# Transposes of a unit's probabilities moved from the head of a step into the middle of its projection piece, in a two-block transformer kernel

## The chip, the cores and the metric

The kernel runs on one core of one Trainium2 chip. The metric is the device time of one execution in microseconds (us), here the median of 3 runs. A core has five engines that run their own instruction streams in order and wait for each other through semaphores: TensorE (PE in the rows; PEld is its weight load), VectorE (DVE), ScalarE (ACT), GpSimd (POOL) and the queues that issue DMA (SP above all).

## What is computed

Two blocks run one behind the other on a sequence of 512 tokens with 1024 features, each of two layers. The first block (feed-forward, pool, Fourier and differential-attention mixer, feed-forward) isn't touched by the change. A layer of the second block, `hybrid_layer`, cut to what matters:

```python
h = rms_norm(x, norm_g)
proj = einsum('btd,de->bte', h, w_in)      # a_q a_k a_v a_g, b_q b_k b_v b_g, m_q m_g
qa, ka = rope(rms_norm(a_q)), rope(rms_norm(a_k))      # 6 heads of 64
oa = moba_attention(qa, ka, a_v)
ob = dilated_attention(qb, kb, b_v)                    # 6 heads
om = memory_attention(qm, km, m_v)                     # 4 heads over 256 memory rows
y = concatenate([oa * silu(a_g), ob * silu(b_g), om * silu(m_g)])
return x + einsum('bte,ed->btd', y, w_out)
```

At 512 tokens both masked kinds of attention come down to scores plus an additive mask, a softmax over the keys, and a product with the values.

## The kernel before

All activations are held feature-major in SBUF. Every large product is made of three matmuls of split fp32 (`three`, lines L458, L459, L460: high by high, high by low, low by high), each 128 rows by 512 tokens. The weights come as a stream of panels of 128 x 2048 through two slots: the DMA fills `raw`, ScalarE copies it into `w_hi` (L945), GpSimd subtracts that into `w_lo` (L450), TensorE waits for the quarters of a panel.

The second block's attention is a software pipeline, `run_stages`. The heads go by groups (stages): stage 1 holds the memory heads, stages 2 to 7 a pair of heads each. A stage has 8 steps. A unit is one block of 128 queries for two heads: the memory stage has 8 units, one in each step; a pair stage has 4, of 128, 256, 384 and 512 keys, which begin in the steps 0, 2, 4 and 6. Each engine walks the same steps in order, and in a step does different parts of different units:

- TensorE, `attention_step`: the scores of this step's unit (L755); the outputs of a group of four units that began three steps ago or more (`LAG_OUT`, L767); the transposes of the unit that began two steps ago (`LAG_TR`, L805; 2, 4, 6 or 8 of them of 128 x 128), into PSUM banks of their own; then `produce(s)`, the step's share of the projections of later groups: four times `three`, 12 matmuls, and in the steps 2 and 3 two matmuls more that sum squares (L840, L841).
- ScalarE, `attention_step`: the copy of the transposed probabilities out of PSUM into `pt` (L1232), which waits for the transposes; in a pair stage the scaling of the probabilities into `att2` (L1240), for the unit that began one step ago (`LAG_ATT`); the exponentials (L1252) of this step's unit; then, in certain steps, copies of queries and keys with their squares (`key_out` in step 0, `query_out` in step 7), the split of a weight panel (L945), square roots (L969, L971), and silu (L1220, L1275). Exponential, root and silu need a table load of their own between them.
- VectorE: the row maximum of the scores (L1638, or L1645 with the mask), the reciprocals (L1667), in the memory stage the scaling into `att2` (L1671), the rotation, the norm of queries and keys, and the gates.

What orders the units is written out by hand as waits. In the memory stage the scores of a unit (L755) wait for the exponentials of the unit before (`t_exp`), which read the same two PSUM banks; in a pair stage they wait for its maximum (`t_max`). The first pair unit behind the memory stage waits for `t_exp` too. In all stages the transposes wait for `t_att`, the copy on ScalarE waits for the transposes (`t_tr`), and the outputs wait for the copy (`t_thi`).

In the stages 1 to 5 `produce` projects gate and value (steps 0 to 3) and query and key (steps 4 to 7) of groups ahead in halves of a chunk, `halves`. In stage 6 there is only gate and value left, in quarters (6 matmuls a step); in stage 7 `beside_last` begins the output projection, and four more steps, `tail`, end the pipeline.

Of the 32 units of a layer, 23 have their transposes in the stages 1 to 5: 8 memory units, and 15 of pairs (the fourth unit of the pair in stage 5 has its transposes in step 0 of stage 6). With two layers that is 46.

Of the kernel before, what the change touches and what calls it, by code (L numbers as in the profile page):

```python
# [152 lines left out]
def ends_group(u):  # L153
    return u % TB == TB - 1
# [58 lines left out]
def build(nc, x, mem, stream, vecs, consts, dist, masks, recip, rope, out):  # L213
    ctx = ExitStack()
    with ctx:  # L215
# [97 lines left out]
        def const(i):  # L313
            return cst[:, i * P:(i + 1) * P]
# [140 lines left out]
        def _(pe):  # L455
# [314 lines left out]
            def attention_step(here, before, s, produce):  # L770
                unit = lagged(here, before, s, 0)
                if unit:
                    stage, u = unit
                    if s == 0 and not here.memory:
                        pe.wait_ge(hn_out, GROUPS * here.l + here.gi + 1)
                    if u and stage.memory:
                        pe.wait_ge(t_exp, stage.u0 + u)
                    elif not stage.memory:
                        pe.wait_ge(t_exp if u == 0 and before.memory else t_max, stage.u0 + u)
                    scores(stage, u).then_inc(t_scores, 1)  # L780
                unit = lagged(here, before, s, LAG_OUT)
                if unit and ends_group(unit[1]):
                    stage, u = unit
                    pe.wait_ge(t_thi, stage.u0 + u + 1)
                    if not stage.memory:
                        pe.wait_ge(v_thi, 7 * stage.l + stage.gi)
                    elif u >= TB:
                        pe.wait_ge(t_y, stage.outs0 + 1)
                    outputs(stage, u).then_inc(t_o, 1)
                unit = lagged(here, before, s, LAG_TR)  # L790
                if unit:
                    stage, u = unit
                    pe.wait_ge(t_att, stage.u0 + u + 1)
                    if not stage.memory:
                        pe.wait_ge(t_thi, stage.u0 + u)
                    elif u >= 2:
                        pe.wait_ge(t_thi, stage.u0 + u - 1)
                    for h in range(2):
                        for kb in range(stage.widths[u] // P):
                            if stage.memory:  # L800
                                n = 256 * h + P * kb
                                dst, src = ps[:, 2 + u % 2, n:n + P], att2[:, h, 256 * (u % 2) + P * kb:256 * (u % 2) + P * kb + P]
                            else:
                                dst, src = ps[:, 2 + h, P * kb:P * kb + P], att2[:, h, P * kb:P * kb + P]
                            mm = pe.transpose(dst, src, const(C_ID))  # L805
                    mm.then_inc(t_tr, 1)
                if produce:
                    produce(s)
                if here and not here.memory and s == 3:
                    pe.wait_ge(v_in, 7 * here.l + here.gi)  # L810
                    pe.wait_ge(t_y, GROUPS * here.l + here.gi)
                    for tb in range(TB):
                        mm = pe.transpose(ps[:, 5, P * tb:P * tb + P],
                                          hraw[:, 0, P * tb:P * tb + P], const(C_ID))
                    mm.then_inc(v_tr, 1)
# [12 lines left out]
            def producer(l, gi):  # L828

                base = BASE2 + LAYER2_PANELS * l  # L830
                G = GROUPS * l + gi + 1
                p_gv = base + 2 * (gi + 1) + 1
                p_qk = base + 2 * (gi + 2)
                more = gi + 2 < GROUPS
                halves = [range(KB // 2), range(KB // 2, KB)]
                quarters = [range(KB // 4 * i, KB // 4 * (i + 1)) for i in range(4)]

                def mean(j):
                    pe.wait_ge(hn_lo, 12 * l + 2 * (gi - 1) + j + 1)
                    pe.matmul(ps[:, 7, :], half_r[:], sq_hi[:, j, :], start=True, stop=False)  # L840
                    pe.matmul(ps[:, 7, :], half_r[:], sq_lo[:, j, :], start=False, stop=True).then_inc(hn_mm, 1)  # L841

                def step(s):
                    if gi == 1 and s == 0:
                        pieces(p_gv - 1, 1, 4, range(KB))
                    if s == 0 and not more:
                        pe.wait_ge(hn_in, 2 * G + 1)
                    if s == 2:
                        pe.wait_ge(hn_in, 2 * G + 2)
                    if not more:  # L850
                        pieces(p_gv, s // 4, (6, 4)[s // 4], quarters[s % 4])
                    elif s < 4:
                        pieces(p_gv, s // 2, (7, 4)[s // 2], halves[s % 2])
                    else:
                        if s == 6:
                            pe.wait_ge(v_in, 7 * l + gi + 1)
                        pieces(p_qk, s // 2 - 2, (6, 4)[s // 2 - 2], halves[s % 2])
                    if s == 2:
                        if more:
                            pe.wait_ge(gate_raw, 7 * l + gi + 1)  # L860
                        mean(0)
                    if s == 3:
                        pe.wait_ge(hn_ms, 2 * G + 1)
                        mean(1)
                return step

            def stack2(l):
                n = 3 * LAYERS + l
                p0 = BASE2 + LAYER2_PANELS * l
                g0 = GROUPS * l  # L870
                pe.wait_ge(memh_ready, 8 * (l + 1))
                for c in range(4):
                    pe.wait_ge(x_ready, 8 * n + DONE_ORDER.index(c) + 1)
                    mem_chunk(c, p0, mh_hi, mh_lo, 256)
                for j in range(2):
                    head_mean(g0, j, 256)
                pe.wait_ge(h_ready, 8 * n + KB)
                mem_chunk(0, p0 + 2, h_hi, h_lo, T)
                pe.wait_ge(square_sum, n + 1)
                mm = pe.matmul(ps[:, 6, :], const(C_MEAN), y[:, 0, :], start=True, stop=True)  # L880
                if l == 0:
                    mm = pe.matmul(ps[:, 4, :], const(C_MEAN), prob2[:, 1, :], start=True, stop=True)
                mm.then_inc(mean_ready, 1)
                mem_chunk(1, p0 + 2, h_hi, h_lo, T)
                pe.wait_ge(hn_ms, 2 * g0 + 2)
                head_mean(g0 + 1, 0, T)
                pe.wait_ge(v_in, 7 * l + 1)
                mem_chunk(2, p0 + 2, h_hi, h_lo, T)
                head_mean(g0 + 1, 1, T)
                pe.wait_ge(scale_in, l + 1)  # L890
                for c in range(2):
                    for tb in range(2):
                        mm = pe.transpose(ps[:, 4, 256 * tb + P * c:256 * tb + P * c + P],
                                          hraw[:, c, P * tb:P * tb + P], const(C_ID))
                mm.then_inc(v_tr, 1)
                mem_chunk(3, p0 + 2, h_hi, h_lo, T)
                pieces(p0 + 4, 0, 6, range(KB))
                pe.wait_ge(hn_out, g0 + 2)
                pe.wait_ge(v_thi, 7 * l + 1)
                def tail(s):  # L900

                    if s > 3:
                        return
                    g = s // 2
                    if s == 0:
                        pe.wait_ge(t_max, UNITS2 * (l + 1))
                    for i in range(4) if s % 2 == 0 else range(4, KB - 1):
                        part(p0 + 2 * GROUPS, i // 2)
                        pe.wait_ge(y_ready, 8 * l + i + 1)
                        project(0, g, 0, Y_ORDER[i], i)  # L910

                def beside_last(s):

                    if s >= 2:
                        part(p0 + 2 * GROUPS + 1, s // 2 - 1)
                        pe.wait_ge(y_ready, 8 * l + s - 1)
                        for g in range(2):
                            project(1, g, 1, Y_ORDER[s - 2], s - 2)

                run_stages(l, attention_step, producer, beside_last, tail)  # L920
                project_out(p0 + 2 * GROUPS, 0, lambda i: pe.wait_ge(y_ready, 8 * l + i + 1), Y_ORDER,
                            (KB - 1, STEPS - 2, 0, 0))
# [1008 lines left out]
```

## Time and profile before

| | |
|---|---|
| Median of 3 runs | 2494.14 us (2491.28 to 2494.87) |
| The profiled execution: span, the only time recorded for it | 2491.6 us |
| TensorE matmuls busy | 2430.0 us, 98% of the span |
| ScalarE busy | 1008.0 us, 40% |
| VectorE busy | 1176.3 us, 47% |
| GpSimd busy | 1121.9 us, 45% |
| Second block's pipelines | about 1910 to 2142 us, and 2219 to 2452 us |

The table is a mean over the whole program, four fifths of which is the first block. No time of the profiled execution is recorded beside its span of 2491.6 us, which lies 2.5 us under the median of the runs. In the rows below, a time is the start of an instruction from the start of the span, and the next number is how long it took. A matmul's own time (0.39) is its latency; what it costs in a stream is the distance of its start to the next one's start.

### The profile page before, as it was taken

What the parts mean: (1) busy time and instruction counts of PE and PEld (TensorE: products, weight loads), DVE (VectorE), ACT (ScalarE), POOL (GpSimd) and SP (SyncE); (2) the same over time, 40 slices, a digit from 0 to 9 for tenths busy, and PEclk for the clock granted to TensorE, in tenths of its full rate; (3) what the DMA queues carried; (4) which work ended last, traced back from release to release, by engine and by line L of the source; (5) the groups of instructions that cost most, each with busy time, mean ns of one, the idle gap of its engine ahead of it and who ended that gap; (6) DMA issues with size and microseconds to landing.
All of it is one profiled execution on the core that took longest, in us unless ns stands there. A gap on an engine that the chain in (4) does not pass through costs nothing.

```text
span 2491.6 us, 30091 instructions
## 1 busy us (share of the span) xinstructions
PE 2430.0 (98%) x10934; PEld 1922.1 (77%) x10934; DVE 1176.3 (47%) x1805; ACT 1008.0 (40%) x1545; POOL 1121.9 (45%) x828
## 2 busy tenths in 40 slices
PE   9999999999999999999999999999999998999988
PEld 7888888668888888888888668888887676776756
DVE  6444115574555105555025665555036655466552
ACT  5333223453222124222133544222235877357772
POOL 5455445325554544555445425555444233343333
PEclk9999999999999999999999999999999999999999
DMA  4222223203222222222223212222232222132212
GB/s 174 101 87 98 102 102 117 85 34 112 90 101 101 93 93 102 94 91 101 102 85 134 72 55 94 101 101 87 99 135 96 78 85 64 68 109 66 85 64 85
DMA packets 37529, 233.18 MB, mean 94 GB/s; under 512 B 5184, under 2 KB 5312, under 8 KB 10816
## 3 DMA queue, kind: packets, MB, share of 16 engines
q1 hardware_dynamic: 36000, 226.51, 26.3%
q10 hardware_dynamic: 1440, 5.45, 0.6%
q8 instruction: 60, 0.98, 0.2%
q14 instruction: 29, 0.24, 0.0%
HBM read 223.55 MB, written 2.10 MB: 91 GB/s over the span
## 4 chain that ended last, share of the span: by engine, by line
issue 58%; POOL 42%; POOLq 1%
POOL w_lo L450 42%; POOLq L444 0%; POOLq L448 0%; POOLq L215 0%; POOLq L450 0%; POOLq L1922 0%
## 5 line engine op out<-in xcount | busy, mean ns | idle before, releaser
L450 POOL TENSOR_TENSOR w_lo<-raw,w_hi 128x512 fp32r<-128x512 f32 x824 | 1121.7, 1393 | 1369.1 <-ACT w_hi L945 1369.0
L458 PE MATMUL ps<-h_hi,w_hi 128*128 128x512 f32 x2304 | 916.4, 398 | 17.1 <-DVE h_lo L1368 10.8
L945 ACT ACTIVATE w_hi<-raw 128x1024 fp32r<-128x1024 f32 x412 | 413.7, 1053 | 1206.6 <-PE ps L460 1199.8
L460 PE MATMUL ps<-h_hi,w_lo 128*128 128x512 f32 x2304 | 900.2, 391 | 0.0
L459 PE MATMUL ps<-h_lo,w_hi 128*128 128x512 f32 x2304 | 899.6, 390 | 0.0
L458 PEld LDWEIGHTS ps<-h_hi,w_hi 128*128 128x128 f32 x2304 | 433.7, 188 | 118.1 <-POOL w_lo L450 11.8
L460 PEld LDWEIGHTS ps<-h_hi,w_lo 128*128 128x128 f32 x2304 | 433.6, 188 | 92.2
L459 PEld LDWEIGHTS ps<-h_lo,w_hi 128*128 128x128 f32 x2304 | 433.9, 188 | 89.9 <-issue 3.4
L460 PE MATMUL ps<-hid_hi,w_lo 128*128 128x512 f32 x704 | 274.1, 389 | 0.0
L459 PE MATMUL ps<-hid_lo,w_hi 128*128 128x512 f32 x704 | 274.1, 389 | 0.0
L458 PE MATMUL ps<-hid_hi,w_hi 128*128 128x512 f32 x704 | 274.1, 389 | 0.0
L1421 DVE SCALAR_TENSOR_TENSOR x_sb<-ps,x_sb 128x512 f32<-128x512 f32 x64 | 43.5, 685 | 410.1 <-PE ps L460 410.1
L1440 DVE TENSOR_TENSOR sq<-hraw,sq 128x512 f32<-128x512 f32 x88 | 142.0, 1613 | 133.2 <-ACT hraw L1054 133.2
L1436 DVE TENSOR_TENSOR hraw<-ps,guess 128x512 f32<-128x512 f32 x88 | 60.8, 691 | 261.8 <-PE ps L460 261.0
L459 PEld LDWEIGHTS ps<-hid_lo,w_hi 128*128 128x128 f32 x704 | 132.2, 188 | 27.6
L460 PEld LDWEIGHTS ps<-hid_hi,w_lo 128*128 128x128 f32 x704 | 132.2, 188 | 27.5
L458 PEld LDWEIGHTS ps<-hid_hi,w_hi 128*128 128x128 f32 x704 | 132.2, 188 | 27.1
L1368 DVE TENSOR_TENSOR hid_lo<-sq,hid_hi 128x512 f32 (+1 forms) x88 | 126.4, 1436 | 12.6 <-issue 0.2
L1442 DVE CAST hid_hi<-sq 128x512 f32 (+1 forms) x88 | 107.8, 1225 | 14.7 <-issue 14.4
L805 PEld LDWEIGHTS ps<-cst,att 128*128 128x128 f32 x304 | 32.5, 141 | 49.4 <-ACT att L1240 28.6
L1232 ACT ACTIVATE pt<-ps 128x256 f32<-128x256 f32 (+2 forms) x64 | 43.2, 675 | 62.8 <-PE ps L805 62.8
L805 PE MATMUL ps<-cst,att 128*128 128x128 f32 x304 | 47.6, 286 | 19.0 <-ACT att L1240 16.8
(242 smaller groups left out, 2034.4 us busy)
## 6 DMA issues: line engine op xcount, KB each, us to landing
raw<-in_stream SPq DMA_DIRECT2D x206, 1024.0 KB, 4.8
hraw<-xs SPq DMA_DIRECT2D x96, 64.0 KB, 2.0
x_sb<-in_x SPq DMA_DIRECT2D x4, 512.0 KB, 8.1
out_x<-x_sb SPq DMA_DIRECT2D x8, 256.0 KB, 2.7
mem_sb<-in_mem ACTq DMA_DIRECT2D x1, 1024.0 KB, 4.7
rec_sb<-in_recip ACTq DMA_DIRECT2D x2, 512.0 KB, 5.0
memn<-in_mem ACTq DMA_DIRECT2D x1, 1024.0 KB, 5.1
dist_sb<-in_dist ACTq DMA_DIRECT2D x2, 448.0 KB, 3.0
```

The lines of the kernel that those rows point to most:

```text
L450: gp.tensor_tensor(w_lo[:, s, c], raw[:, s, c], w_hi[:, s, c].bitcast(F32), ALU.subtract).then_inc(lo_split, 1)
L458: pe.matmul(dst, l_hi, r_hi, start=first, stop=False)
L459: pe.matmul(dst, l_hi, r_lo, start=False, stop=False)
L460: return pe.matmul(dst, l_lo, r_hi, start=False, stop=last)
L805: mm = pe.transpose(dst, src, const(C_ID))
L945: act.activation(w_hi[:, s, c], raw[:, s, c], ACT.Copy).then_inc(hi_split, 1)
L1232: act.activation(pt[:, :, 0:kbs, P * b:P * b + P], src, ACT.Copy).then_inc(t_thi, 1)
L1368: return dve.tensor_tensor(dst, src, hi.bitcast(F32), ALU.subtract)
L1421: dve.scalar_tensor_tensor(out=x_sb[:, m, :], in0=ps[:, m, :], scalar=scale, in1=x_sb[:, m, :], op0=ALU.mult, op1=ALU.add).then_inc(x_read ...
L1436: dve.tensor_tensor(hraw[:, e, :], ps[:, 2 * e, :], rstd, ALU.mult).then_inc(gate_in, 1)
L1440: dve.tensor_tensor(sq[:, e, :], hraw[:, e, :], sq[:, e, :], ALU.mult)
L1442: dve.tensor_copy(hid_hi[:, c, :], sq[:, e:e + 1, :])
```

## The change

TensorE's transposes of a unit become a function, `turn`, that is handed to `produce`. In the stages 1 to 5 (`more`) `produce` calls it behind the first two of the step's four groups of three matmuls. In stage 6, in stage 7 (`beside_last`) and in the `tail` it is called first, which is where the transposes stood. No instruction is added or taken away, and no other engine's code is touched.

```diff
-                if unit:
+
+                def turn():
+                    if not unit:
+                        return
                     stage, u = unit
                     pe.wait_ge(t_att, stage.u0 + u + 1)
...
                     mm.then_inc(t_tr, 1)
+
                 if produce:
-                    produce(s)
+                    produce(s, turn)
+                else:
+                    turn()
...
                     if not more:
+                        turn()
                         pieces(p_gv, s // 4, (6, 4)[s // 4], quarters[s % 4])
                     elif s < 4:
-                        pieces(p_gv, s // 2, (7, 4)[s // 2], halves[s % 2])
+                        ks = halves[s % 2]
+                        pieces(p_gv, s // 2, (7, 4)[s // 2], ks[:2])
+                        turn()
+                        pieces(p_gv, s // 2, (7, 4)[s // 2], ks[2:])
                     else:
                         if s == 6:
                             pe.wait_ge(v_in, 7 * l + gi + 1)
-                        pieces(p_qk, s // 2 - 2, (6, 4)[s // 2 - 2], halves[s % 2])
+                        ks = halves[s % 2]
+                        pieces(p_qk, s // 2 - 2, (6, 4)[s // 2 - 2], ks[:2])
+                        turn()
+                        pieces(p_qk, s // 2 - 2, (6, 4)[s // 2 - 2], ks[2:])
```

On TensorE, step 6 of the memory stage begins with the scores (L755), then outputs (L767), and before the change went on with the transposes (L805) of the unit of step 4:

```order
L755 MATMUL ps<-km,mq 128x256 x2
L767 MATMUL ps<-pt,vm 64x512 x4
L805 MATMUL ps<-cst,att 128x128 x4
L458 MATMUL ps<-h_hi,w_hi 128x512
L459 MATMUL ps<-h_lo,w_hi 128x512
L460 MATMUL ps<-h_hi,w_lo 128x512
```

The same place on TensorE in the changed kernel, where the transposes have the line L808:

```order
L755 MATMUL ps<-km,mq 128x256 x2
L767 MATMUL ps<-pt,vm 64x512 x4
L458 MATMUL ps<-h_hi,w_hi 128x512
L459 MATMUL ps<-h_lo,w_hi 128x512
L460 MATMUL ps<-h_hi,w_lo 128x512
L458 MATMUL ps<-h_hi,w_hi 128x512
L459 MATMUL ps<-h_lo,w_hi 128x512
L460 MATMUL ps<-h_hi,w_lo 128x512
L808 MATMUL ps<-cst,att 128x128 x4
L458 MATMUL ps<-h_hi,w_hi 128x512
L459 MATMUL ps<-h_lo,w_hi 128x512
L460 MATMUL ps<-h_hi,w_lo 128x512
```

The transposes have moved past six projection matmuls; the other six of the step follow them.

On TensorE again, step 6 of a pair stage begins with the scores of the unit with 512 keys (`ps<-qk 128x512`), followed before the change by the six transposes of the unit with 384 keys:

```order
L755 MATMUL ps<-qk 128x512 x2
L805 MATMUL ps<-cst,att 128x128 x6
L458 MATMUL ps<-h_hi,w_hi 128x512
L459 MATMUL ps<-h_lo,w_hi 128x512
L460 MATMUL ps<-h_hi,w_lo 128x512
```

In the changed kernel the same place on TensorE reads:

```order
L755 MATMUL ps<-qk 128x512 x2
L458 MATMUL ps<-h_hi,w_hi 128x512
L459 MATMUL ps<-h_lo,w_hi 128x512
L460 MATMUL ps<-h_hi,w_lo 128x512
L458 MATMUL ps<-h_hi,w_hi 128x512
L459 MATMUL ps<-h_lo,w_hi 128x512
L460 MATMUL ps<-h_hi,w_lo 128x512
L808 MATMUL ps<-cst,att 128x128 x6
```

Here too they stand six matmuls later. ScalarE's order is the same in both kernels.

## Rows read from the trace of the kernel before

**Rows 1.** The page: span, and busy time of each engine.

```profile
span 2491.6 us, 30091 instructions
PE 2430.0 (98%) x10934; PEld 1922.1 (77%) x10934; DVE 1176.3 (47%) x1805; ACT 1008.0 (40%) x1545; POOL 1121.9 (45%) x828
```

**Rows 2.** TensorE's waits (us, times, longest): stages 2-5 of each layer; whole span.

```profile
PE ps L805 <- ACT att L1240: 2.8, 7, 0.7
...
PE ps L805 <- ACT att L1240: 2.5, 7, 0.4
...
PE ps L805 <- DVE att L1671: 2.2, 4, 0.9
```

**Rows 3.** Timeline of TensorE, memory stage, layer 0: start, took, [idle before <-releaser].

```profile
1928.68 0.50 PE L840 MATMUL ps<-sq_hi,half_r 128*128 128x512 f32 x1 [0.75 <-DVE y L1717]
...
1929.97 0.66 PE L805 MATMUL ps<-cst,att 128*128 128x128 f32 x4
1930.38 0.48 PE L458 MATMUL ps<-h_hi,w_hi 128*128 128x512 f32 x1
...
1931.86 0.39 PE L458 MATMUL ps<-h_hi,w_hi 128*128 128x512 f32 x1
...
1933.79 0.70 PE L755 MATMUL ps<-km,mq 64*128 64x256 f32 x4
1934.43 0.66 PE L805 MATMUL ps<-cst,att 128*128 128x128 f32 x4
...
1943.37 0.70 PE L755 MATMUL ps<-km,mq 64*128 64x256 f32 x4 [1.27 <-ACT prob L1252]
...
1945.87 0.66 PE L805 MATMUL ps<-cst,att 128*128 128x128 f32 x4
...
1949.54 0.70 PE L755 MATMUL ps<-km,mq 64*128 64x256 f32 x4 [0.27 <-ACT prob L1252]
...
1953.51 0.49 PE L755 MATMUL ps<-qk 64*128 64x128 f32 x4
```

**Rows 4.** Timeline of ScalarE, memory stage, layer 0: start, took, idle before.

```profile
1930.67 0.60 ACT L1232 ACTIVATE pt<-ps 128x512 f32<-128x512 f32 x1
...
1932.58 0.48 ACT L1252 ACTIVATE prob<-ps,nmx 128x256 f32<-128x256 f32 x1
...
1935.38 0.59 ACT L1232 ACTIVATE pt<-ps 128x512 f32<-128x512 f32 x1
...
1940.40 0.58 ACT L1232 ACTIVATE pt<-ps 128x512 f32<-128x512 f32 x1
...
1946.56 0.60 ACT L1232 ACTIVATE pt<-ps 128x512 f32<-128x512 f32 x1 [1.31 <-PE ps L805]
...
1950.87 0.60 ACT L1232 ACTIVATE pt<-ps 128x512 f32<-128x512 f32 x1 [1.38 <-PE ps L805]
1951.36 0.47 ACT L1252 ACTIVATE prob<-ps,nmx 128x256 f32<-128x256 f32 x1
```

**Rows 5.** Timeline of TensorE, stages 4 to 5 of layer 0.

```profile
2043.62 0.87 PE L805 MATMUL ps<-cst,att 128*128 128x128 f32 x6 [0.42 <-ACT att L1240]
...
2050.67 1.09 PE L805 MATMUL ps<-cst,att 128*128 128x128 f32 x8 [0.27 <-ACT att L1240]
...
2054.45 1.73 PE L767 MATMUL ps<-pt,vp 128*64 128x512 f32 x8
```

**Rows 6.** Timeline of ScalarE, stages 4 to 5 of layer 0.

```profile
2036.70 0.60 ACT L1232 ACTIVATE pt<-ps 128x512 f32<-128x512 f32 x1 [0.33 <-PE ps L805]
...
2052.04 1.03 ACT L1232 ACTIVATE pt<-ps 128x1024 f32<-128x1024 f32 x1
```

**Rows 7.** Two stretches: us, ScalarE busy (instructions), granted clock, DMA share, GB/s.

```profile
1935.38:1943.30 7.92, 7.79 (x15) 1.00 0.31 103
2036.70:2043.56 6.86, 6.76 (x12) 1.00 0.31 85
```

**Rows 8.** Timeline of TensorE, step 0 of stage 6, layer 0.

```profile
2083.38 1.09 PE L805 MATMUL ps<-cst,att 128*128 128x128 f32 x8 [0.26 <-ACT att L1240]
```

More of the change, by code:

```diff
@@ L841, in mean, with step @@
                     pe.matmul(ps[:, 7, :], half_r[:], sq_lo[:, j, :], start=False, stop=True).then_inc(hn_mm, 1)
-                def step(s):
+                def step(s, turn):
                     if gi == 1 and s == 0:
@@ L899, in stack2, with tail @@
                 pe.wait_ge(v_thi, 7 * l + 1)
-                def tail(s):
+                def tail(s, turn):
+                    turn()
                     if s > 3:
@@ L910, in tail, with beside_last @@
                         project(0, g, 0, Y_ORDER[i], i)
-                def beside_last(s):
+                def beside_last(s, turn):
+                    turn()
                     if s >= 2:
```

## The prediction, made before the changed kernel ran

> **What bounds the kernel now.** I read the page first: TensorE's matmuls cover 2430.0 of 2491.6 us, ScalarE is busy for 40% of the span [rows 1]. That says that TensorE sets the end nearly everywhere, so a microsecond that TensorE loses or gains in the second block's pipelines is one of the kernel's time. It does not say that ScalarE has room where it is needed: 40% is a mean over a program of which the first block is four fifths.
>
> Then TensorE's waits. The transposes (L805) wait for the scaled probabilities of ScalarE, in the pair stages that the change touches 2.8 us in one layer and 2.5 us in the other, 7 times each, and for those of VectorE 2.2 us over the whole span, in the memory stages [rows 2]. These 7.5 us are what transposes issued later could spare; the large waits of the same kind lie in the stages 6 and 7, where they stay ahead.
>
> Then the timelines, engine by engine, to see who is late for whom. In the memory stage the scores of step 6 wait 1.27 us for ScalarE's exponentials, those of step 7 wait 0.27 us [rows 3]; and ScalarE, in the same steps, idles 1.31 and 1.38 us until the transposes are there [rows 4]. So a ring is closed in each memory step: TensorE's transposes, ScalarE's copy (L1232), ScalarE's exponentials behind it in its queue, TensorE's next scores. The exponentials need nothing of the transposes; they only stand behind the copy. In a pair stage the ring is longer. From the copy at 2036.70 to the transposes at 2043.62 ScalarE is busy 6.76 of 6.86 us [rows 7], and the idle time that opens this stretch, 0.33 us, ended with the transposes [rows 6]. The granted clock is 1.00 in both stretches [rows 7], the higher level, 2.4 GHz, and I take it to stay there.
>
> **How far the transposes move.** Six projection matmuls pass ahead of them. From the first behind a block of fp32 matmuls to the seventh it is 1930.38 to 1931.86, 1.48 us [rows 3]. Each moved unit has its transposes 1.48 us later in its step. Two prices follow: what is spared where TensorE waited for the probabilities, and what is lost where ScalarE waited for the transposes.
>
> **Memory stage, step 2: spared, but not kept.** Here TensorE waited for VectorE's probabilities (the longest such wait, 0.9 us, rows 2). That goes. But the two matmuls at the end of the same step (L840) wait 0.75 us for VectorE's gate [rows 3], whose time rests on VectorE's own queue. It is late next, and it takes the gain: 0.
>
> **Memory stage, step 3.** Transposes from 1929.97 to 1931.45. The copy starts 0.69 us behind the start of four transposes (1945.87 to 1946.56, rows 3 and 4): 1932.14, where it was 1930.67. From such a copy to the next scores, with the exponentials' table load between, it is 2.97 us (1940.40 to 1943.37) or 2.98 us (1946.56 to 1949.54). So the scores of step 4 start at 1935.12 and not at 1933.79: **+1.33**. ScalarE's exponentials were just in time before, 1932.58 plus 1.07 being 1933.65.
>
> **Steps 4 and 5.** Transposes 0.64 us behind the scores (1933.79 to 1934.43) plus 1.48: 1937.24, copy at 1937.93 where it was 1935.38. From that copy to the next, 5.02 us (1935.38 to 1940.40), ScalarE does exponentials and both root activations without a gap: 7.79 us busy of the 7.92 to the end of step 5's exponentials [rows 7]. Nothing there absorbs. Scores of step 6: 1937.93 + 5.02 + 2.97 = 1945.92, where they were 1943.37, so 2.55 in all: **+1.22**.
>
> **Step 6.** Its transposes move by 1.48 and ScalarE was idle until they came (1.31 us, rows 4), with the table load behind: **+1.48**.
>
> **Step 7.** Before, TensorE's own work set the length, 1949.54 to 1953.51, 3.97 us. The ring is now 0.63 scores, 1.48, 0.69 to the copy, 0.49 to the exponentials (1950.87 to 1951.36, rows 4), and 1.07 from there to scores (2.98 less the 1.91 from copy to exponentials, 1930.67 to 1932.58): 4.36, and the first pair unit's scores wait for it: **+0.39**. The memory stage loses 4.4 us a layer. Bounds: 1.48 if step 6 alone is exposed, 5.9 if all of four steps are in full.
>
> **Pair stages 2 to 5.** In step 4 the copy comes 1.48 us later, since its wait ended with the transposes. ScalarE has no gap from there to the probabilities that step 6's transposes wait for, so these come 1.48 later. TensorE too reaches those transposes 1.48 us later. The wait of 0.42 [rows 5] is there again, not spared, and so is the one of 0.27 in step 0 of the next stage, as ScalarE's queue stays late until it next has to wait for a panel of TensorE in step 3. Gain 0; bounds, a gain of the whole 5.3 us of rows 2, or a loss of 1.48 at one place in each of eight stages.
>
> Next in line are the outputs (L767): the copy of the fourth unit, 2052.04 with 1.03 us, ends at 2053.07 [rows 6], 1.38 us ahead of the outputs at 2054.45 [rows 5]. Moved by 1.48 it is 0.1 too late. Taken at four places in a layer (stages 2 to 5): **+0.4**, bounds 0 and 4 times 1.0, if ScalarE's copy of the memory stage's last unit, whose slack I take from this row, has none.
>
> **Stage 6, step 0.** Here the transposes of stage 5's last unit are still issued first. They waited 0.26 us before [rows 8]. ScalarE arrives 1.48 later out of stage 5, TensorE doesn't: **+1.5** a layer, bounds 0 and 1.5.
>
> **The seam.** Each moved block cuts the stream of projection matmuls once more. The distance 1.48 holds the price of one entry behind fp32 work; the later half of the piece pays it again, but the transposes no longer follow other fp32 work. Bounds 0 and 0.11 a unit (1.48 less six at 0.228 from the rhythm of the rows 3, an estimate), I take 0.05, exposed only where TensorE doesn't wait for ScalarE in the same step, some five units a layer: **+0.25**.
>
> **The sum.** 4.4 + 0.4 + 1.5 + 0.25 = 6.55 us a layer, 13.1 for two. The profiled execution goes from 2491.6 to 2504.7; the median stood 2.5 us above its span, so 2494.1 + 13.1 = 2507.2 us, slower by 0.5%.
>
> **A rule against this forecast.** The profile gives TensorE 98% and ScalarE 40% [rows 1]. The Trainium skill, Perfetto Trace Analysis, Optimization Strategy, says to find the gaps on the most-contended engine, see which semaphore they wait for and make that dependency start sooner or end faster, and its section on the most-contended engine takes occupancy as the measure for ScalarE. By that reading the gaps ahead of the transposes are the thing to close, ScalarE with 40% has room, and the sum would be the first rival's below. Rows 7 disagree for the stretch that matters: ScalarE is busy 98% of it.
>
> **Rivals.**
> *Faster: the waits are spared.* TensorE's waits of 2.8, 2.5 and 2.2 us [rows 2] go, 46 seams at 0.05 cost 2.3 at most: 5.2 us, 2488.9. For it: those waits are there, and 1.48 us is more than each of them. It decides on the copy: if a copy that comes 1.48 us later doesn't delay ScalarE's exponentials (it had to have that much slack), it wins. Against it: ScalarE's waits of 0.33, 1.31 and 1.38 us are all for the transposes themselves. Chance 0.08.
> *No change.* The delays of ScalarE are taken up by something I read as tight (a copy that starts before all transposes are over, the gate's wait in step 2), and leave one exposed step of 1.48 a layer, against some spared wait: 2494 to 2498. Chance 0.07.
> *Half of it.* The memory stage's ring as forecast, but no loss at stage 6, or the reverse: 4.4 or 1.5 for the layer plus seams, 2498.5 to 2504.5. Chance 0.1.
> *Worse.* ScalarE's lateness reaches the weight splits, then GpSimd and the panels, or each moved unit exposes its 1.48: 15 more units at 0.5 to 1 us, 2515 to 2522. Against it: the split in step 3 waits for TensorE, not for ScalarE's queue. Chance 0.05.
>
> **How the numbers follow.** The forecast has 0.7. A change under 0.2% (5 us) can't be told from none here. Slower: 0.7 + 0.05 + 0.1, faster 0.08, same 0.07. The range runs from 2500 (memory rings at half their price, stage 6 unharmed) to 2512 (seams exposed in full for 46 units, 5 us more than taken).
>
> **What the changed kernel's profile would show.** Right: waits of L755 on ScalarE's exponentials in the memory stage in steps 4, 5, 6, 7 and in the first pair step, 1.3 us and more in step 4, and from step 4's scores to the first pair unit's 22.8 us instead of 19.7 (1933.79 to 1953.51); the waits of the transposes in the stages 2 to 5 unchanged near 0.3 to 0.4; 1.7 us in step 0 of stage 6; ScalarE idle 1.8 us ahead of the copy in step 4. Wrong: those waits of the transposes gone and no new ones at L755, or losses at L458 for panels.

## The result, and the profile after

The changed kernel takes 2514.36 us (median of 4 runs, 2511.99 to 2517.34), the kernel before 2493.09 (4 runs, the earlier three among them): ratio 1.009, 95% interval 1.0077 to 1.0103. It is slower by 21 us, where 13 were forecast; the range ended at 2512. The profiled execution is the fastest of the four, with a span of 2510.2 us, 18.6 more than before.

The page of the changed kernel, which answers to [rows 1]:

```profile
span 2510.2 us, 30087 instructions
PE 2442.3 (97%) x10934; PEld 1925.8 (77%) x10934; DVE 1175.0 (47%) x1805; ACT 1007.4 (40%) x1545; POOL 1117.8 (45%) x828
```

The work is the same; TensorE's busy time is 12 us more, and the other 6 of the 18.6 are idle. Its waits over the whole span (us in total, times, longest):

```profile
PE ps L755 <- ACT prob L1267: 10.7, 9, 2.2
PE ps L808 <- ACT att L1255: 10.5, 16, 3.1
PE ps L808 <- ACT sq_hi L1214: 6.3, 2, 3.2
...
PE ps L846 <- DVE y L1732: 3.3, 2, 1.7
```

One wait has grown, that of the scores for ScalarE's exponentials, from 3.1 to 10.7 us, and one is new, 6.3 us of the transposes for ScalarE's squares of a query, `sq_hi`. VectorE's probabilities are no longer waited for (2.2 us in [rows 2]). What that spared turned up as the wait of L846 for the gate, 3.3 us (L840 in the kernel before, 1.5 us), as the prediction said for step 2.

The memory stage of layer 0 on TensorE, answering to [rows 3]; the steps 4, 6 and 7 and the first pair unit begin with these scores:

```profile
1935.22 0.70 PE L755 MATMUL ps<-km,mq 64*128 64x256 f32 x4 [1.16 <-ACT prob L1267]
...
1945.86 0.70 PE L755 MATMUL ps<-km,mq 64*128 64x256 f32 x4 [2.21 <-ACT prob L1267]
...
1953.50 0.70 PE L755 MATMUL ps<-km,mq 64*128 64x256 f32 x4 [1.63 <-ACT prob L1267]
...
1957.91 0.49 PE L755 MATMUL ps<-qk 64*128 64x128 f32 x4 [0.29 <-ACT prob L1267]
```

From 1935.22 to 1957.91 it is 22.7 us, where it was 19.7; the forecast was 22.8. ScalarE in the same stage, answering to [rows 4]:

```profile
1932.23 0.60 ACT L1247 ACTIVATE pt<-ps 128x512 f32<-128x512 f32 x1 [1.42 <-PE ps L808]
...
1937.98 0.60 ACT L1247 ACTIVATE pt<-ps 128x512 f32<-128x512 f32 x1 [0.92 <-PE ps L808]
...
1950.52 0.60 ACT L1247 ACTIVATE pt<-ps 128x512 f32<-128x512 f32 x1 [2.77 <-PE ps L808]
...
1956.26 0.60 ACT L1247 ACTIVATE pt<-ps 128x512 f32<-128x512 f32 x1 [2.80 <-PE ps L808]
```

These are the copies of steps 3, 4, 6 and 7. Each now ends a wait for the transposes, and TensorE's next scores wait for the exponentials behind that copy: both engines idle in turn.

Step 0 of stage 6, layer 0, on TensorE, answering to [rows 8]:

```profile
2088.19 0.49 PE L755 MATMUL ps<-qk 64*128 64x128 f32 x4
2091.86 1.92 PE L808 MATMUL ps<-cst,att 128*128 128x128 f32 x8 [3.17 <-ACT sq_hi L1214]
2093.42 0.78 PE L458 MATMUL ps<-h_hi,w_hi 128*128 128x512 f32 x1
```

The transposes wait 3.17 us, where 0.26 was before and 1.7 forecast, and not for their probabilities. The matmul at 2093.42 takes 0.78 us where such a one took 0.48 [rows 3]. That is the clock; stretches of the changed kernel, with us, busy times, granted clock, DMA share and GB/s:

```profile
1935.20:1957.90 22.70, 18.37 (x88) 11.98 (x89) 13.50 (x27) 16.03 (x30) 5.13 (x4) 1.00 0.13 47
2262.30:2277.20 14.90, 13.27 (x49) 7.71 (x49) 4.92 (x13) 6.51 (x14) 0.00 (x0) 0.77 0.00 0
2088.20:2099.80 11.60, 8.43 (x43) 5.69 (x42) 3.46 (x11) 9.18 (x19) 1.63 (x2) 0.85 0.13 32
2407.00:2419.60 12.60, 9.42 (x43) 6.04 (x42) 3.46 (x11) 9.21 (x19) 2.54 (x3) 0.73 0.15 36
```

The first is the memory stage of layer 0, at 1.00; the second the end of layer 1's, steps 6 and 7, at 0.77, a mean of stretches at 2.4 and at 1.2 GHz; the last two hold step 0 of stage 6 in either layer. Laying the starts of the scores (L755) of both kernels beside each other, step by step, gives where the time went, in us:

| | layer 0 | layer 1 | forecast, each |
|---|---|---|---|
| Memory stage, steps 3 to 7 | +4.3 | +7.1 | +4.4 |
| Stages 2 to 5 | +1.2 | +0.8 | +0.65 |
| Stage 6, step 0 | +3.8 | +4.7 | +1.5 |
| Stages 6 and 7, behind that | -2.2 | -1.1 | 0 |
| Sum | +7.1 | +11.5 | +6.55 |

### The profile page after: what moved, and what is told of

It reads as the page before. It is cut to its first block, busy times and chain, and to the rows that moved or that the text cites. A ratio compares the mean times of both kernels' runs of the same rounds, so it can differ in the third digit from the quotient of the medians.

```text
span 2510.2 us, 30087 instructions
## 1 busy us (share of the span) xinstructions
PE 2442.3 (97%) x10934; PEld 1925.8 (77%) x10934; DVE 1175.0 (47%) x1805; ACT 1007.4 (40%) x1545; POOL 1117.8 (45%) x828
## 4 chain that ended last, share of the span: by engine, by line
issue 58%; POOL 41%; POOLq 1%
POOL w_lo L450 41%; POOLq L444 0%; POOLq L448 0%; POOLq L215 0%; POOLq L450 0%; POOLq L1937 0%
## 5 line engine op out<-in xcount | busy, mean ns | idle before, releaser
L808 PE MATMUL ps<-cst,att 128*128 128x128 f32 x304 | 48.8, 293 | 17.1 <-ACT att L1255 10.5
L1376 DVE SCALAR_TENSOR_TENSOR newt<-ms,newt 128x512 f32<-128x512 f32 (+1 forms) x30 | 29.4, 978 | 76.5 <-ACT newt L986 42.8
```

## The experiments

Theory: the loss is a ring of waits (TensorE's transposes, ScalarE's copy, ScalarE's exponentials, TensorE's scores), with two additions that the prediction lacked, a wait that the transposes of stage 6 were moved behind, and the clock. Rival: moving a block of transposes into a stream of matmuls costs by itself, for every moved unit alike (the seam), and that is where the 21 us come from. Times are medians; each ratio is to the kernel before on the same chip.

**Memory units alone.** All pair units' transposes stand at the head again.

```diff
+                if unit and not unit[0].memory:
+                    turn()
+                    unit = None
                 if produce:
                     produce(s, turn)
```

> Only the 16 memory units' transposes stand in the middle of the piece; those of all pair units stand ahead again, in stage 6 ahead of the wait for the squares too. Ring theory (ScalarE's exponentials stand behind the copy that waits for the transposes): the memory stages lose what they lost in the changed kernel, 4.3 us in layer 0 and 4.3 to 7.1 in layer 1, depending on whether the granted clock drops: 9 to 13 us above before in all. Seam theory (each move costs by itself, the same for every unit): 16 of 46 units, a third of 21 us, 7 us above before, spread evenly.

2508.82 us, ratio 1.0061 (1.0048 to 1.0075), 15.6 us above before: a third of the units makes three quarters of the loss. That speaks against the seam, though it is also more than the 13 that I had expected at most. In its profile the stages 2 to 6 are as before to 0.3 us in layer 0; the memory stages lose 8.4 and 8.9 us. The granted clock (the number ahead of the last two) in three stretches of layer 0's:

```profile
1929.00:1936.40 7.40, 6.51 (x26) 4.55 (x24) 4.19 (x10) 4.63 (x9) 0.00 (x0) 0.77 0.46 154
1936.40:1947.00 10.60, 8.20 (x42) 5.70 (x42) 8.57 (x14) 9.53 (x17) 5.12 (x4) 1.00 0.29 99
1947.00:1953.00 6.00, 6.00 (x23) 2.61 (x23) 2.75 (x7) 1.82 (x2) 0.00 (x0) 0.72 0.01 3
```

In this execution the clock fell in layer 0 as well, where the changed kernel's profile has it at 1.00.

**Pair units alone.** The same edit with the condition turned round.

> Only the 30 pair units' transposes stand in the middle; the memory units' are ahead again. Ring theory: the memory stages are as before; what is left is the drift in stages 2 to 5 (0.7 to 1.2 us a layer) and step 0 of stage 6 (3.8 to 4.7, of which 1 to 2 come back in stages 6 and 7): 5 to 9 us above before. Seam theory: 30 of 46 units, 14 us above before.

2502.03 us, ratio 1.0042 (1.0028 to 1.0055), 8.9 above before; its profiled execution is the fastest, 4.9 above before in its span. TensorE's waits in the memory stage of layer 0 are those of before:

```profile
PE ps L755 <- ACT prob L1270: 1.5, 2, 1.3
PE ps L808 <- DVE att L1689: 1.1, 2, 0.9
PE ps L849 <- DVE y L1735: 0.8, 1, 0.8
```

The stages 2 to 5 lose 0.8 us in layer 0 and 0.3 in layer 1, stage 6's step 0 loses 2.2 and 3.7. So 30 units cost less than 16, and most of it in one step of which the transposes weren't to be moved. The two kernels add up to 24.5 us, more than the 21.3 of both moves together, so these shares are good to some 3 us.

This kernel also lets the seam be read: in a step where TensorE waits for nothing in either kernel, what a moved unit adds is its price. Steps 4 and 5 of stage 2 (layer 0) are such steps. The scores at their start and at their end, before and in this kernel:

```profile
1970.28 0.92 PE L755 MATMUL ps<-qk 64*128 64x384 f32 x4
1977.19 1.13 PE L755 MATMUL ps<-qk 64*128 64x512 f32 x4
```

```profile
1970.56 0.92 PE L755 MATMUL ps<-qk 64*128 64x384 f32 x4
1977.56 1.13 PE L755 MATMUL ps<-qk 64*128 64x512 f32 x4
```

6.91 us and 7.00. In the stages 2 to 5 of both layers this distance is 0.06 to 0.09 us longer in all seven profiles with moved pair units, and in the others it is that of before. So a seam costs 0.06 to 0.09 us, at most 4 us for 46 units and not 21.

**Stage 6's transposes ahead of the wait.** Looking for `sq_hi` in the rows above led to the code: in step 0 of stage 6 `produce` first waits for the squares of a query (`hn_in`), and only then calls `turn`. So it isn't so that `turn` comes first there, where the transposes stood, as the section on the change has it. In step 2 it stands behind such a wait too, but no time was lost there: the waits for `sq_hi` are two, one in step 0 of either layer.

```diff
+                    if not more:
+                        turn()
                     if s == 0 and not more:
                         pe.wait_ge(hn_in, 2 * G + 1)
...
                     if not more:
-                        turn()
                         pieces(p_gv, s // 4, (6, 4)[s // 4], quarters[s % 4])
```

> The changed kernel, with the transposes in stage 6 issued ahead of TensorE's wait for the squares of the query (hn_in) and not behind it. If that wait is why stage 6 lost 3.8 to 4.7 us where 1.5 was forecast: the step costs 1.5 again, the total falls by 4 to 6 us against the changed kernel, to 15 to 17 above before. If ScalarE's lateness alone makes the loss there, or the clock: no change, 21 above before.

2511.72 us, ratio 1.0077 (1.0064 to 1.0091): 2.6 us less than the changed kernel, and not the 4 to 6 expected. The intervals of the two overlap. Its profile was also unlucky in layer 0: the memory stage, which this edit doesn't touch, lost 8.8 us where the changed kernel's lost 4.3, with a granted clock of 0.85 over the 34 us from 1929 on. The step itself is clearer, here in layer 0:

```profile
2096.14 1.09 PE L808 MATMUL ps<-cst,att 128*128 128x128 f32 x8 [1.62 <-ACT att L1256]
2097.69 0.80 PE L458 MATMUL ps<-h_hi,w_hi 128*128 128x512 f32 x1 [0.45 <-ACT sq_hi L1215]
```

The transposes wait 1.62 us for their probabilities (1.7 forecast) and no longer for the squares. In layer 1, where the clock stayed at 1.00, the step is 1.35 us longer than before (1.5 forecast); in layer 0, with 0.79 over the 8 us from 2094 on, it is 2.8 longer.

**The wait alone.** The kernel before with one difference, stage 6's transposes behind the wait; in the other stages `turn` is called first, and its calls in the middle of a piece are gone. Against the changed kernel, cut to the call:

```diff
+                    if more:
+                        turn()
                     if s == 0 and not more:
                         pe.wait_ge(hn_in, 2 * G + 1)
...
                     if not more:
                         turn()
                         pieces(p_gv, s // 4, (6, 4)[s // 4], quarters[s % 4])
```

> The kernel before, with one thing changed: in step 0 of stage 6 the transposes stand behind the wait for the squares of the query, not ahead of it. By the profile of before these transposes started at 2083.38 and the squares end at 2084.87: they start 1.5 us later, no longer lie under ScalarE's work, and the step gets 1.0 us longer in each layer, in the profile from the scores of stage 6's first unit to those of its second (7.76 us before in layer 0). If the wait doesn't matter by itself but only with a late ScalarE: 7.8 us again. In the changed kernel this step took 11.6 us.

A single run, 2495.95 us, so only the step is read. From scores to scores it is 0.87 us longer in layer 0 (1.0 expected), where the clock stayed at 1.00, and 2.4 in layer 1, where the granted clock was 0.79 over the 8 us from 2394 on. The wait is there without a late ScalarE (layer 0):

```profile
2086.91 1.09 PE L808 MATMUL ps<-cst,att 128*128 128x128 f32 x8 [1.82 <-ACT sq_hi L1212]
```

Lateness with 1.35 and the wait with 0.87 make 2.2 us of the 3.8 and 4.7; what is left is the clock, as the filled kernel below shows.

**The exponentials ahead of the copy.** TensorE's order is the changed one; in the memory stage ScalarE does the exponentials (L1252 of before) first and the copy (L1232) behind them.

```diff
+                first = here and here.memory
+                if first:
+                    exponentials()
+                turned_out()
...
+                if not first:
+                    exponentials()
```

> The changed kernel with ScalarE's exponentials of a step ahead of its copy of the transposes, in the memory stage alone; TensorE's order is that of the changed kernel. Ring theory: the exponentials no longer wait for the transposes, the 4.3 us and the clock's drop in the memory stages go: 11 to 13 us less than the changed kernel, 8 to 10 above before. Seam theory: nothing changes, 21 above before.

2503.79 us, ratio 1.0044 (1.003 to 1.0057), 10.6 above before and 10.6 under the changed kernel, by the medians: close to the 11 to 13 less that were expected, and a little short of them. From step 3 to the first pair unit, layer 1 loses 0.2 us where the changed kernel lost 7.1, with every transpose still in the middle of its piece. (Layer 0 loses 1.4, with the clock at 0.59 behind the wait for the gate in step 2, see the last section.) TensorE's waits there, steps 3 to 7 of layer 1, first in the changed kernel:

```profile
PE ps L755 <- ACT prob L1267: 5.2, 4, 2.2
PE ps L846 <- DVE y L1732: 1.7, 1, 1.7
```

and in this one:

```profile
PE ps L755 <- ACT prob L1261: 1.7, 1, 1.7
PE ps L846 <- DVE y L1742: 1.7, 1, 1.7
```

Four waits for exponentials became one. This settles the ring in the memory stage against the seam.

**Past 3 matmuls, not 6.** The kernel with memory units alone, and in both branches:

```diff
-                        pieces(p_gv, s // 2, (7, 4)[s // 2], ks[:2])
+                        pieces(p_gv, s // 2, (7, 4)[s // 2], ks[:1])
                         turn()
-                        pieces(p_gv, s // 2, (7, 4)[s // 2], ks[2:])
+                        pieces(p_gv, s // 2, (7, 4)[s // 2], ks[1:])
```

> Memory units' transposes alone are moved, as in the kernel with only those, but past 3 projection matmuls and not 6: 0.80 us later in the step, not 1.48. Ring theory, by its own arithmetic: step 3 0.65, steps 4 and 5 0.55, step 6 0.80, step 7 nothing (3.67 us of ring against 3.97 of TensorE's work): 2.0 us a layer, 4 above before, 6 with some fall of the clock. Seam theory: as many seams as with 6 matmuls, so 15.6 above before again.

2497.92 us, ratio 1.0029 (1.0018 to 1.004), 5.6 above before: within the ring's 4 to 6, and a third of what the same number of seams cost at 6 matmuls. By layers the profile has 1.8 and 1.8 us (2.0 expected). The loss grows faster than the shift (0.80 against 1.48 us), since part of it is absorbed, as the arithmetic of the ring has it, and since the clock stayed at 1.00 in these stages of the profile.

**Idle time filled.** The changed kernel, with matmuls that nobody reads where TensorE stood idle longest.

```diff
+                    if stage.memory and s >= 6:
+                        pe.wait_ge(hn_ms, 2 * GROUPS * here.l + 6)
+                        for i in range((8, 6)[s - 6]):
+                            pe.matmul(ps[:, 7, :], half_r[:], h_hi[:, i, :], start=True, stop=True)
...
                     if s == 0 and not more:
+                        pe.wait_ge(hn_ms, 2 * G)
+                        for i in range(12):
+                            pe.matmul(ps[:, 7, :], half_r[:], h_hi[:, i % KB, :], start=True, stop=True)
                         pe.wait_ge(hn_in, 2 * G + 1)
```

> The changed kernel with matmuls that nobody reads, in the places where TensorE stands idle: 8 ahead of the scores of step 6 and 6 ahead of those of step 7 of the memory stage, 12 ahead of the wait for the squares in step 0 of stage 6. Their outputs go to a bank that is free there. If the longer waits cost a second time, because the granted clock falls to 1.2 GHz behind them: the clock stays at 1.00 in these stretches, and the time falls by 3 to 6 us against the changed kernel, to 13 to 17 us above before. If the clock has no part in it: 21 above before or a little more, for the added matmuls.

2508.49 us, ratio 1.0069 (1.0055 to 1.0082): 5.9 less than the changed kernel by the medians, 5.2 by the ratios, of which the intervals still touch, and 16.2 above before (13 to 17 expected). It does more work and takes less time. The mean granted clock of its five runs is 0.996 or 0.997, that of the changed kernel's four 0.992 to 0.994. The stretches of above, in this kernel:

```profile
2262.30:2277.20 14.90, 14.30 (x70) 9.67 (x71) 6.72 (x22) 8.12 (x18) 0.00 (x0) 1.00 0.02 6
...
2088.00:2099.80 11.80, 11.54 (x63) 7.69 (x64) 4.71 (x17) 9.78 (x21) 2.74 (x3) 1.00 0.16 39
2407.00:2419.60 12.60, 12.37 (x65) 8.41 (x64) 6.56 (x19) 9.88 (x23) 4.76 (x4) 1.00 0.18 44
```

All at 1.00. The memory stages lose 4.3 us in both layers (the ring's 4.4), and step 0 of stage 6 loses 2.2 and 2.1, the sum of the two parts measured apart. So 2.8 us of layer 1's memory stage and 1.6 and 2.6 us of stage 6 were the clock. The two profiles are only 3.5 us apart, for two reasons: behind step 0 of stage 6 the filled kernel regains 1.0 us, where the changed kernel regained 3.3; and in stage 5 of layer 1 it has a wait of 1.3 us for the gate that the changed kernel's profile lacks. Why that wait comes in some profiles isn't known.

**The same order on ScalarE, without the move.** The kernel before, with the exponentials first in all stages. Against the edit of the kernel with the exponentials ahead:

```diff
-                first = here and here.memory
+                first = True
```

> The kernel before, transposes at the head of the step, with ScalarE's exponentials ahead of its copy of the transposes in every stage. Ring theory: TensorE's waits for exponentials in the memory stage (1.5 us a layer) go and the pair stages' waits for probabilities (0.7 us a stage) shrink: 4 to 8 us under before. If the copy is then late for the outputs it gives that back: no change.

2492.56 us, ratio 1.0002 (0.9993 to 1.0011): no change, a miss. The waits of the transposes in the pair stages (2.8 us in [rows 2]) did not shrink:

```profile
PE ps L805 <- ACT att L1262: 3.9, 4, 1.2
```

They became fewer and longer, one a stage. In the memory stage the longer wait, 1.3 us in step 6, is left too. I had expected the copy alone to stand in the way; ScalarE's two root activations stand there as well, ahead of the exponentials. That reading rests on the program's order and [rows 7] and wasn't tried.

**Both delays removed.** The exponentials first everywhere, and stage 6's transposes ahead of the wait, with the changed order on TensorE: the edits of the kernel with stage 6's transposes ahead of the wait and of the last one together.

> The changed order on TensorE, in stage 6 ahead of the wait for the squares, with ScalarE's exponentials ahead of its copy in every stage: both delays of the changed kernel removed. Ring theory: no ring is left, what the move spares comes through, and the time is that of the kernel before with the same order on ScalarE or 1 to 3 us less, so 4 to 9 us under before. If moving the transposes costs in itself: above that kernel by 5 us or more.

2490.8 us, ratio 0.9992 (0.9983 to 1.0001): the 21 us are gone, all of them, with the 46 blocks still in the middle. It is 1.8 us under the kernel before with the same order on ScalarE (1 to 3 expected), but not 4 us under before. Its memory stage of layer 0 has a stretch at the low clock behind the wait for the gate:

```profile
1929.40:1933.60 4.20, 4.20 (x16) 3.00 (x15) 3.17 (x9) 4.16 (x7) 0.00 (x0) 0.59 0.79 266
```

**The pair units alone, with both delays removed.** The last kernel, with the memory units' transposes at the head.

```diff
+                if unit and unit[0].memory:
+                    turn()
+                    unit = None
                 if produce:
                     produce(s, turn)
```

> The kernel with both delays removed (transposes in stage 6 ahead of the wait, ScalarE's exponentials ahead of its copy), but with the memory units' transposes at the head of the step again, so that only the pair units' stand in the middle. The profile of its forerunner gained 0.3 to 0.4 us at the end of each pair stage and lost 1.6 us in the memory stage. Ring theory: the gain of eight pair stages stays, some 2 to 3 us under before. Seam theory: 30 seams and nothing spared, 0 to 3 us above before.

2489.56 us, ratio 0.999 (0.9981 to 0.9999), 2.75 us under before, as expected, though the interval ends just short of 1. In the stages 2 to 5 of its profile no wait of the transposes is left in either layer, and each stage is 0.2 to 0.6 us shorter: 1.6 and 1.5 us a layer, of 2.8 and 2.5 us of waits that are gone [rows 2]. The seams of 15 units are most of the difference. Its median is the lowest of the study; from the kernel with both delays removed it can't be told apart.

## Why the prediction was wrong, point by point

**Direction and mechanism: right.** TensorE sets the end, ScalarE's copy waits for the transposes and holds up its exponentials. Turning those two about on ScalarE took 10.6 us off, with TensorE's order left as changed.

**Memory stage, 4.4 us a layer: right where the clock held.** 4.3 in layer 0, and 4.3 in both layers with the idle time filled. Step by step: 1.3 at step 4 (1.33 forecast), 1.06 at step 6 (1.22), 1.47 at step 7 (1.48), 0.44 at the first pair unit (0.39). The gain in step 2 was lost to the gate's wait, as said. Of the signs named, the 22.8 us came as 22.7; but step 5's scores waited only 0.20 us, and ScalarE idled 0.92 us ahead of the copy in step 4, not 1.8.

**The clock: the step that failed.** "I take it to stay there" was taken from stretches in which TensorE waited at most 1.3 us at a time. The waits that follow from my own sums are longer, 1.27 plus 1.22 us ahead of step 6's scores and 1.7 in stage 6 (measured: 2.21 and 3.17), and behind them the clock fell to 1.2 GHz in some places. So the sum had nothing for a term that was 7 us in the profiled execution (2.8, 1.6 and 2.6); over the runs it is 5 to 6 by the filled kernel, which at 2508.5 us would have lain in the range. The trace of before had the warning, in stage 6 of layer 0, behind a longer wait:

```profile
2104.66 1.31 PE L805 MATMUL ps<-cst,att 128*128 128x128 f32 x6 [3.33 <-ACT att L1240]
2105.62 0.78 PE L458 MATMUL ps<-h_hi,w_hi 128*128 128x512 f32 x1
...
2104.70:2108.50 3.80, 3.80 (x13) 3.23 (x14) 3.55 (x9) 3.77 (x4) 0.00 (x0) 0.55 0.00 0
```

The Trainium skill, TensorE: Matmul & The Clock Gate, Part 1 (The HAM clock gate), has the clock fall when the array goes idle and rise when it is busy again. The runs here agree: the same stretches had 0.77, 0.85 and 0.73 with the idle time in them and 1.00 with it filled.

**Stage 6, 1.5 us a layer: the second step that failed.** The lateness of ScalarE was there with 1.35. "Here the transposes of stage 5's last unit are still issued first" was wrong: they are issued first of the matmuls, but behind the wait for the squares. That cost 0.87 more, and the clock's 1.6 and 2.6 came behind the longer wait. The order of the rows without their waits doesn't show it; the diff does.

**Given back: not in the sum.** Stages 6 and 7 regained 2.2 and 1.1 us. TensorE waits there for ScalarE's probabilities anyway, and behind step 0 of stage 6 those waits shrank from 10.9 to 8.8 us over both layers; no run tries this by itself.

**Pair stages and seams: nearly right, by luck.** The stages 2 to 5 lost 1.2 and 0.8 us against 0.65, but the terms are off both ways. The waits of the transposes for their probabilities were forecast to stay; they fell from 2.8 and 2.5 us a layer [rows 2] to 1.0 and 0.7. The one of 0.42 us in stage 4 [rows 5] is 0.16 in the changed kernel:

```profile
2050.37 0.88 PE L808 MATMUL ps<-cst,att 128*128 128x128 f32 x6 [0.16 <-ACT att L1255]
```

The late outputs waited 0.2 us a layer, not 0.4. Against that stand the seams: 0.06 to 0.09 us each, where 0.05 was taken, and in all of the 15 pair units, where five units a layer were taken. By an estimate from the measured seam that makes some 1.2 us a layer; what else ate up the spared waits isn't resolved.

**The sum again.** From the 13.1 us of the forecast to the 18.6 of the profiled execution: the clock +7.0, the wait in stage 6 +1.3, the stages 2 to 5 +0.7, the memory stages -0.2, given back -3.3. That the miss isn't larger is luck too, a gain that I hadn't seen against losses that I hadn't seen. The medians are 21.3 apart; the profiled execution is the fastest of the four, with a mean granted clock of 0.994, and the other three have 0.993, 0.992 and 0.992.

**The rule against the forecast** (the Trainium skill, Perfetto Trace Analysis, Optimization Strategy) speaks of making the dependency start sooner or end faster. The change did neither: it let the waiting work come later. By that the gaps did shrink, as the first rival had it, and the kernel still became slower by 21 us, since the rival's own condition failed: ScalarE's exponentials had no slack behind the copy.

**The range** was built from bounds of the single terms. It had nothing for the clock or for stage 6 beyond 1.5 us a layer, and ended 2.4 us too low.

## What to carry to other kernels

Before work is moved later on one engine, look at who waits for it, and at what is queued behind that wait and doesn't need it: here the exponentials were held up by a copy, and that cost more than the 7.5 us of waits that the move could spare. Read every moved instruction against the waits that it passes, not only against the instructions. Where a forecast makes TensorE wait longer than any wait in the trace that left the clock alone, the clock belongs in the range.

## What the runs showed of the hardware

The granted clock fell behind some waits and not behind others of the same length. Behind the wait of 1.65 us for the gate (L846), in the memory stage of layer 0, the changed kernel's profile kept 1.00, and the kernel with the exponentials ahead of the copy in that stage had 0.59 in the 4.2 us that follow. The same stretch in the one and the other:

```profile
1929.40:1933.60 4.20, 4.20 (x22) 3.23 (x22) 3.23 (x8) 2.75 (x4) 0.00 (x0) 1.00 0.78 266
```

```profile
1931.00:1935.20 4.20, 4.20 (x16) 2.79 (x15) 2.93 (x9) 4.16 (x7) 0.00 (x0) 0.59 0.80 259
```

That same wait of 1.65 us stands in both layers of the six profiles in which the memory units' transposes are six matmuls later, and behind five of the twelve the clock fell. Two waits of 1.77 us, in step 6 of the kernel past 3 matmuls, left it at 1.00. Where the steps could be laid beside an execution at full clock, a fall cost 1.2 to 1.7 us, in one place 2.6. Behind the waits of before in the pipelines' stages 1 to 5, 1.3 us and less, the granted clock was 1.00 from 1910 to 2082.6 us and from 2219.5 to 2392 us.

What decides between a fall and none stays open. The time of an execution goes roughly with its mean granted clock: of the eleven runs of the kernel with both delays removed, the three with a mean granted clock of 0.998 took 2488.4 to 2489.4 us, the four with 0.995 took 2492.0 to 2494.1.
